# Rotary scores from high and low halves, the mask product first, the value product after the rotary scores

## What is computed

```python
def block(args):
    ql, qr, qp = args
    s = (jnp.einsum('bqhc,bkc->bhqk', ql, c, preferred_element_type=jnp.float32)
         + jnp.einsum('bqhr,bkr->bhqk', qr, kr, preferred_element_type=jnp.float32))
    s = s * ks[:, :, None, :] * scale
    s = jnp.where(k_pos[None, None, None, :] <= qp[None, None, :, None], s, NEG_INF)
    p = jax.nn.softmax(s, axis=-1).astype(c.dtype)
    return jnp.einsum('bhqk,bkc->bqhc', p, c)
...
o = jnp.einsum('bshc,chv->bshv', o, w_uv).reshape(bsz, s_q, N_HEADS * V_DIM)
return o @ w_o
```

## Time and profile before

| | |
|---|---|
| median of 3 runs | 2081.05 us |
| the three runs | 2082.86, 2081.05, 2073.68 us |
| the profiled execution, its own time | 2079.41 us |
| its span in the trace | 2077.7 us |
| busy share of the span: PE, DVE, ACT, POOL | 99%, 77%, 53%, 16% |
| granted TensorE clock, mean | 0.998 |
| sample stage, from the first turned page to the first scores | 1473.6 to 1499.5 us |
| heads, from the first scores to the last rotary scores | 1499.5 to 1674.4 us, with the projection from 1582.6 to 1628.9 us in them |

### The profile page before, as it was taken

The page is one execution under the profiler, slowest core; times in us unless marked ns, Lnnn a source line. Parts: engine busy times, 40 slices in busy tenths (PEclk is TensorE's granted clock), DMA queues, the critical chain, the costliest instruction groups (busy, mean ns, idle before and its releaser), DMA issues.

```text
span 2077.7 us, 44241 instructions
## 1 busy us (share of the span) xinstructions
PE 2058.9 (99%) x16692; PEld 1993.7 (96%) x16692; DVE 1601.1 (77%) x2667; ACT 1103.1 (53%) x1898; POOL 341.7 (16%) x384
## 2 busy tenths in 40 slices
PE   9999999999999999999999999999999999999999
PEld 8999999999999999999999999998768789999998
DVE  6779885437367998988899898678665468989987
ACT  5446554443225655645665665445564346655555
POOL 0011111221011111111211111111122121111111
PEclk9999999999999999999999999999999999999999
DMA  5467783322224777775777777441322127777775
GB/s 162 121 160 179 187 200 105 91 92 80 84 81 114 176 180 179 180 182 151 172 179 181 187 183 172 138 134 29 96 72 82 61 62 158 178 189 171 198 175 129
DMA packets 362555, 293.57 MB, mean 141 GB/s; under 512 B 21591, under 2 KB 329092, under 8 KB 362148
## 3 DMA queue, kind: packets, MB, share of 16 engines
q1 hardware_dynamic: 326266, 226.84, 36.4%
q0 software_dynamic: 35824, 64.37, 19.1%
q10 hardware_dynamic: 314, 0.37, 0.1%
HBM read 224.57 MB, written 2.66 MB: 109 GB/s over the span
## 4 chain that ended last, share of the span: by engine, by line
PE 85%; DMA 8%; DVE 4%; issue 2%; ACT 1%; SPq 1%; ACTq 0%; DVEq 0%
PE side L825 26%; PE main L776 26%; PE main L825 19%; DMA raw<-raw 3%; DMA sums_w<-raw 2%; PE side L1370 2%; DMA raw<-in_ffn_w_gate 2%; PE main L1130 2%; PE main L1300 1%; DVE w_lo L2104 1%; DMA raw<-in_ffn_w_up 1%; PE side L1340 1%; PE side L1220 1%; PE main L1200 1%; PE side L1044 1%
## 5 line engine op out<-in xcount | busy, mean ns | idle before, releaser
L825 PE MATMUL side<-xw_hi,w_hi 128*128 128x260 f32 x1344 | 381.1, 284 | 5.1 <-ACT main L1545 1.5
L825 PE MATMUL side<-xw_hi,w_lo 128*128 128x260 f32 x1344 | 381.0, 283 | 0.0
L825 PE MATMUL side<-xw_lo,w_hi 128*128 128x260 f32 x1344 | 380.1, 283 | 0.0
L2104 DVE TENSOR_TENSOR w_lo<-raw,w_hi 128x512 fp32r<-128x512 f32 (+2 forms) x472 | 323.4, 685 | 35.5 <-ACT w_hi L1490 16.6
L825 PE MATMUL main<-xw_hi,w_hi 128*128 128x260 f32 x1008 | 286.1, 284 | 0.0
L825 PE MATMUL main<-xw_lo,w_hi 128*128 128x260 f32 x1008 | 284.7, 282 | 0.0
L825 PE MATMUL main<-xw_hi,w_lo 128*128 128x260 f32 x1008 | 284.5, 282 | 0.0
L825 PEld LDWEIGHTS side<-xw_hi,w_hi 128*128 128x128 f32 x1344 | 253.2, 188 | 8.5 <-ACT main L1545 3.0
L825 PEld LDWEIGHTS side<-xw_hi,w_lo 128*128 128x128 f32 x1344 | 253.2, 188 | 0.0
L825 PEld LDWEIGHTS side<-xw_lo,w_hi 128*128 128x128 f32 x1344 | 252.8, 188 | 0.0
L2104 DVE TENSOR_TENSOR w_lo<-sums_w,w_hi 128x1024 fp32r<-128x1024 f32 (+1 forms) x232 | 218.6, 942 | 1.0 <-ACT w_hi L1473 1.0
(11 more groups left out here) (460 smaller groups left out, 5340.8 us busy)
## 6 DMA issues: line engine op xcount, KB each, us to landing
sums_w<-raw POOLq DMA_DIRECT2D x112, 256.0 KB, 3.3
raw<-raw POOLq DMA_DIRECT2D x112, 256.0 KB, 5.1
raw<-in_ffn_w_gate SPq DMA_DIRECT2D x86, 256.0 KB, 4.4
raw<-in_ffn_w_gate SPq DMA_DIRECT2D x43, 512.0 KB, 5.9
raw<-in_ffn_w_up SPq DMA_DIRECT2D x84, 256.0 KB, 4.5
raw<-in_ffn_w_up SPq DMA_DIRECT2D x42, 512.0 KB, 6.2
raw<-in_gmlp_w_in SPq DMA_DIRECT2D x16, 1024.0 KB, 5.3
raw<-in_ffn_w_down SPq DMA_DIRECT2D x56, 256.0 KB, 4.1
```

What stands on the lines that cost most here:

```text
L825: mm = nc.tensor.matmul(into[j], w_tiles(w, weights_at(s, j))[:, k, :], moving[:, k, order[j], :], start=(j in (0, 1) and k == 0 and i == ...
L2104: a = nc.vector.tensor_tensor(dst, src, hi.bitcast(F32), ALU.subtract)
```

## The change

The change does the following.

- The rotary scores are made of three fp32r products as the latent ones are. For that there are `kr_hi`, `kr_lo` (the keys, once) and `rope_hi`, `rope_lo` (the queries, once for two heads, all 128 partitions). `rope_lo` takes the place of `qr` in memory, tile by tile.
- `qr_moved` is filled by SP with two DMAs for two heads (partitions 0 to 63 to 64 to 127 and back), where ACT copied 64 partitions in each head. ACT makes `rope_hi` by two copies and POOL `rope_lo` by two subtractions for two heads.
- The first two moves stand on SP ahead of the last 16 page DMAs, the third ahead of the first loads of `w_o`, and the others among the loads of `key_scale`.
- The mask product comes first in each bank.
- The value product comes after all scores of a head, on PE; on DVE the value tile is copied after the maxima.
- A few tiles and semaphores are placed anew (`ks_rows`, `kr_lo`, `c_squared`), which moves no work.

Cut to what matters (the second part of a move, the tiles and the renamed semaphores are left out):

```diff
+            def move_rope(r_):
+
+                if r_ >= 2:
+                    sp.wait_ge(rope_lo_set, 2 * r_ - 2)
+                if r_ >= 1:
+                    sp.wait_ge(qr_moved_set, 32 * r_)
+                for lo in (0, ROPE):
+                    sp.dma_start(qr_moved[lo:lo + ROPE, r_ % 2, :], qr[ROPE - lo:P - lo, r_, P:3 * P]).then_inc(qr_moved_set, 16)
+
             sp.wait_ge(kn_done, 17)
+            sp.wait_ge(qr_set, H // 2)
+            move_rope(0)
+            move_rope(1)
             load_pages(10, 14)
...
             sp.wait_ge(os_done, 2)
+            move_rope(2)
             load_out(0)
             load_out(1)
             for h in range(2, H):
                 spread_scales(h)
+                if h % 2 == 0 and h + 4 < H:
+                    move_rope(h // 2 + 2)
...
+                for blocks in ((2, 3), (0, 1)) if h == 0 else ((0, 1, 2, 3),):
+                    if h == 0 and 0 in blocks:
+                        pe.wait_ge(sd_set, 3)
+                    for q in blocks:
+                        if free is not None and q % 2 == 0:
+                            pe.wait_ge(evac_done, free - 1 + q // 2)
+                        if h >= 1:
+                            pe.wait_ge(score_scaled, QB * (h - 1) + q + 1)
+                        nc.tensor.matmul(main[:, q // 2, q % 2, q * P:(q + 1) * P], mask_ops[:, 0, :], mask_ops[:, 1, :],
+                                         start=True, stop=False, skip_group_check=True)
+                    for q in blocks:
+                        bank = main[:, q // 2, q % 2, :]
+                        nk, cols = (q + 1) * P, slice(q * P, (q + 1) * P)
+                        for a, b in ((q_hi[:, h % 2, cols], c_hi), (q_hi[:, h % 2, cols], c_lo), (q_lo[:, h, cols], c_hi)):
+                            nc.tensor.matmul(bank[:, 0:nk], a, b[:, 0:nk], start=False, stop=False, skip_group_check=True)
+                r_ = h // 2
+                pe.wait_ge(rope_lo_set, 2 * r_ + 2)
+                for pair in ((0, 1), (3, 2)):
+                    for i, (a, b) in enumerate(((rope_hi[:, r_ % 2, :], kr_hi), (rope_hi[:, r_ % 2, :], kr_lo),
+                                                (rope_lo[:, r_, :], kr_hi))):
+                        for q in pair:
...
-                    scores(h, lambda: values(g - 1), free=e if g == KC + 1 else None)
+                    scores(h, free=e if g == KC + 1 else None)
+                if g >= 1:
+                    values(g - 1)
...
+            def round_rope(r_):
+
+                if r_ >= 2:
+                    act.wait_ge(scored, QB * (2 * r_ - 2))
+                act.wait_ge(qr_moved_set, 32 * r_ + 32)
+                nc.scalar.activation(outer_blocks(rope_hi[:, r_ % 2, :]), outer_blocks(qr[:, r_, 0:SEQ]), ACT.Copy)
+                nc.scalar.activation(rope_hi[:, r_ % 2, P:3 * P], qr_moved[:, r_ % 2, :], ACT.Copy).then_inc(rope_hi_set, 1)
...
                 if h + 2 < H:
-                    move_rope(h + 2)
+                    if h % 2 == 0:
+                        round_rope(h // 2 + 1)
                     split_queries(h + 2)
...
-                if g >= 1:
-                    value_tile(g - 1)
                 if h < H:
                     dve.wait_ge(key_scale_in[h % 2], 16 * (h // 2 + 1))
...
+                if g >= 1:
+                    value_tile(g - 1)
                 if g >= 0:
                     dve.wait_ge(prob_turned, 3 * g + 2)
...
+            def rope_rest(r_):
+
+                pool.wait_ge(rope_hi_set, r_ + 1)
+                nc.gpsimd.tensor_tensor(outer_blocks(rope_lo[:, r_, 0:SEQ]), outer_blocks(qr[:, r_, 0:SEQ]),
+                                        outer_blocks(rope_hi[:, r_ % 2, :].bitcast(F32)), ALU.subtract).then_inc(rope_lo_set, 1)
+                nc.gpsimd.tensor_tensor(rope_lo[:, r_, P:3 * P], qr_moved[:, r_ % 2, :],
+                                        rope_hi[:, r_ % 2, P:3 * P].bitcast(F32), ALU.subtract).then_inc(rope_lo_set, 1)
```

More of the change, by code:

```diff
@@ L251, in program @@
         c_lo = sb("c_lo", [P, TOK], F32R, late)
-        qr = sb("qr", [P, H // 2, TOK], F32, late)
+        turned_queries = ExitStack()
+        qr = sb("qr", [P, H // 2, TOK], F32, turned_queries)
+        turned_queries.close()
+        rope_lo = sb("rope_lo", [P, H // 2, TOK], F32R, late)
         wkv = sb("wkv", [P, H, P], F32, late)
@@ L313, in program, with outer_blocks @@
         o_t = sb("o_t", [P, TOK], F32, heads)
+        kr_hi = sb("kr_hi", [P, SEQ], F32R, heads)
+        rope_hi = sb("rope_hi", [P, 2, SEQ], F32R, heads)
         KV_THIRD = -(-H * P // 3)
         qr_moved = rstd_all[:, 0:4 * P].rearrange("p (s c) -> p s c", s=2)
+        def outer_blocks(t):
+            return t.rearrange("p (q c) -> p q c", c=P)[:, 0:QB:QB - 1, :]
         heads.close()
@@ L1269, in _, with scores @@
                     tr.then_inc(ks_turned, 1)
-            def scores(h, between=None, free=None):
+            def scores(h, free=None):
                 if h == 0:
-                    pe.wait_ge(c_lo_set, 1)
+                    pe.wait_ge(c_lo_set, 2)
                     pe.wait_ge(key_parts_set, 2)
                 pe.wait_ge(q_lo_set, h + 1)
-                for q in (2, 3, 0, 1) if h == 0 else range(QB):
-                    if h == 0 and q == 0:
+                for blocks in ((2, 3), (0, 1)) if h == 0 else ((0, 1, 2, 3),):
+                    if h == 0 and 0 in blocks:
@@ L1278, in scores @@
                         pe.wait_ge(sd_set, 3)
-                    if free is not None and q % 2 == 0:
-                        pe.wait_ge(evac_done, free - 1 + q // 2)
-                    if h >= 1:
-                        pe.wait_ge(score_scaled, QB * (h - 1) + q + 1)
-                    bank = main[:, q // 2, q % 2, :]
-                    nk, cols = (q + 1) * P, slice(q * P, (q + 1) * P)
-                    nc.tensor.matmul(bank[:, 0:nk], q_hi[:, h % 2, cols], c_hi[:, 0:nk], start=True, stop=False)
@@ L1286, in scores @@
-                    nc.tensor.matmul(bank[:, 0:nk], q_hi[:, h % 2, cols], c_lo[:, 0:nk], start=False, stop=False)
-                    nc.tensor.matmul(bank[:, 0:nk], q_lo[:, h, cols], c_hi[:, 0:nk], start=False, stop=False)
-                for q in range(QB):
-                    nc.tensor.matmul(main[:, q // 2, q % 2, q * P:(q + 1) * P], mask_ops[:, 0, :], mask_ops[:, 1, :],
-                                     start=False, stop=False, skip_group_check=True)
-                if between is not None:
-                    between()
@@ L1293, in scores @@
-                pe.wait_ge(qr_moved_set, h + 1)
-                for q in (0, 1, 3, 2):
-                    nk = (q + 1) * P
-                    if q in (0, 3):
-                        lo, q_rope = ROPE * (h % 2), qr[:, h // 2, q * P:(q + 1) * P]
-                    else:
-                        lo, q_rope = ROPE - ROPE * (h % 2), qr_moved[:, h % 2, (q - 1) * P:q * P]
-                    nc.tensor.matmul(main[:, q // 2, q % 2, 0:nk], q_rope[lo:lo + ROPE, :],
-                                     kr_t[lo:lo + ROPE, 0:nk], start=False, stop=True).then_inc(scored, 1)
+                    for q in blocks:
[5 more added lines that the diff above has]
+                                         start=True, stop=False, skip_group_check=True)
@@ new lines, in scores @@
+                for pair in ((0, 1), (3, 2)):
+                    for i, (a, b) in enumerate(((rope_hi[:, r_ % 2, :], kr_hi), (rope_hi[:, r_ % 2, :], kr_lo),
+                                                (rope_lo[:, r_, :], kr_hi))):
+                        for q in pair:
+                            lo, nk = ROPE * (h % 2) if q in (0, 3) else ROPE - ROPE * (h % 2), (q + 1) * P
+                            mm = nc.tensor.matmul(main[:, q // 2, q % 2, 0:nk], a[lo:lo + ROPE, q * P:(q + 1) * P],
+                                                  b[lo:lo + ROPE, 0:nk], start=False, stop=(i == 2), skip_group_check=True)
+                            if i == 2:
+                                mm.then_inc(scored, 1)
@@ L1915, in _ @@
             act.wait_ge(evac_done, e + 3)
-            nc.scalar.activation(square[:, 0, :], c_t[:], ACT.Square).then_inc(c_squared, 1)
+            nc.scalar.activation(square[:, 0, :], c_t[:], ACT.Square).then_inc(cq_squared, 1)
             act.wait_ge(rms_mm, at_mla.rms + 3)
@@ L2008, in _ @@
                     nc.scalar.activation(c_hi[:], c_t[:, 0:SEQ], ACT.Copy).then_inc(c_hi_set, 1)
+                if y == 9:
+                    nc.scalar.activation(kr_hi[:], kr_t[:, 0:SEQ], ACT.Copy).then_inc(c_hi_set, 1)
                 if y == 4:
@@ L3165, in _ @@
                     query_rest(h + 2)
+                    if h % 2 == 0:
+                        rope_rest(h // 2 + 1)
             value_rest(H - 1)
```

25 lines of the change are left out of this document (11 added, 14 removed).

## The result

The changed kernel takes 2094.53 us in the median of six runs (2088.77 to 2097.46); the kernel before took 2081.0 us beside it (2073.68 to 2082.86, six runs). The ratio is 1.0076, 95% interval 1.0062 to 1.0089, so the change makes the kernel slower by 0.8%. The forecast was 2085 with a range of 2076 to 2094. The profiled execution took 2095.88 us, its span is 2094.2 us; before it was 2077.7, so 16.5 us are to be found.

What follows compares the result with a forecast made beforehand. PE's own sequence was taken as the bound, other engines counting only where PE waits. Terms of -0.9, +1.2, +1.6, +2.0 and +0.7 gave +4.6 us on 2079.41, 2084.0 (2085.7 by the runs' median); forecast 2085, range 2076 to 2094.

Steps and rivals of the forecast that it cites:

- Rotary scores: PE's rotary stage in each head: three fp32r passes plus 0.1 us for switching, 1.28 becomes 1.06, 0.22 us less.
- The first rival: Array halves don't run side by side for fp32r: rotary stage 2.09 us, +1.0 us in 15 heads, 2100; chance 0.07.
- The rule that the prediction took from the Trainium skill's page: Weight loads overlap running matmuls only from another row group; the rotary stage would take 1.6 us.
- Value tile: PE's last two transposes wait for DVE's copy, weighing starts at T + 2.52; reordering costs 0.15 us per head.
- the maxima end at T + 1.45: On DVE, the third reduction again starts at T + 0.16, so the maxima end at T + 1.45, taken as 1.5.
- T: The moment at which PE leaves a head's rotary scores, 1538.83 in the regular head of the profile before.
- Heads 3 to 6: DVE, with the quarter of `w_lo` in between, is free only at T + 8.0; +1.2 us over four heads.
- the third rival: POOL's new subtractions slow DVE's normalisation; with its room used up, 2.1 us in 6 heads, 2097; chance 0.04.
- SP at the pages: Two moves ahead of the last 16 page DMAs delay them 3.5 us on SP; PE loses 1.6 us.
- SP at head 2: Moves issued first on SP make head 2's key scales late for DVE; heads 1 and 2 together +2.0 us.
- they arrive at 1523.1: Head 2's key scales land at 1523.1 instead of 1522.3, while DVE wants them at 1520.6.
- Head 10: Masks first need all four banks, so PE starts its products only at 1629.96: +0.7 us.

Runs made afterwards that it cites:

- one rotary term less: The changed kernel without the product of the queries' high halves and the keys' low halves in the rotary scores; 2091.28 us, 1.0057.
- the reordering alone: The kernel before with only the value product moved behind the rotary scores on PE and the value tile behind the maxima on DVE; 2084.85 us, 1.0026.

## Why the prediction was wrong

**What bounds the kernel, and the sign.** The forecast of 2085 was slower than before, and the kernel is slower, but "slower" by more than a measurement can tell had a chance of only 0.14, against 0.83 for the same. That PE's own sequence sets the time, and that other engines count only where PE waits, is right for the kernel before. In the new order it failed for the regular heads: each has a wait, and their length is that of a circle over POOL, DVE, PE and ACT that the forecast never summed.

**Rotary scores, "I add 0.1. So 1.28 becomes 1.06".** The halves do run side by side (pairs start as one), and a term costs its columns. The term that was mis-sized is the 0.1 us added to the columns: 0.24 us are fixed. So the stage is 0.06 us shorter and not 0.22. The first rival falls. The rule that the prediction took from the Trainium skill's page "TensorE: Matmul & The Clock Gate", Part 3, "The mechanism", falls too, as it was read there: by it the stage would have taken 1.6 us, and it took 1.22. (The same section also lets a load go ahead into a background weight buffer, which the prediction left out and which the trace doesn't contradict.)

**Value tile, "+0.15", and "the maxima end at T + 1.45".** In head 13, T = 1671.52; the ninth transpose starts at 1673.88 and the weighing at 1674.16, T + 2.64 against my T + 2.52. The size is nearly right; what failed is that I gave the maxima their old 0.17 us. Before, they started after POOL's subtraction had ended (head 6: 1556.36 against 1555.78). With the value tile no longer ahead of them they start inside it. Regular heads became +0.23 instead of -0.07. Along PE's own sequence the difference can be added up, 0.16 in the rotary stage, 0.12 here and the rest at other borders, but that sum is no cause: a stage shorter by another 0.33 us bought nothing (one rotary term less), and the old float32 stage made no head longer (the reordering alone). The step that failed is that PE's terms were added with the maxima ending at T + 1.45; they end when POOL lets them, and the circle through them takes 8.29 us. With POOL's subtraction moved behind them the heads take 8.19.

**Heads 3 to 6.** The step "the quarter of `w_lo` comes in between, and DVE is free at T + 8.0" failed in kind. DVE was free in time: its first reduction starts 0.42 us ahead of T (1556.67 and 1557.09) as in other heads. The quarter delays POOL's `h_lo` by 0.38 us, POOL's next subtraction starts later, and this one holds the maxima. I had the third rival (POOL slows DVE, 0.04) and looked for it at the normalisation, in even heads; it was at the maxima, in twelve of sixteen heads, even and odd, from a subtraction that was there before. (In the old order of the value tile, POOL's new subtractions did hold the maxima, but in odd heads.)

**SP at the pages.** The delay on SP (3.5 forecast; the last page's issue ends at 1487.03 instead of 1483.19, 3.8) and PE's wait (1.6 and 2.01) were nearly right. What was missing is the clock after the wait, 1.7 us.

**SP at head 2.** The step "they arrive at 1523.1" failed, 13.6 us after head 1's start there: the scales left 6.56 us after it (1519.68 and 1513.12) instead of 5.9, flew 9.0 us instead of 7.6, and were there after 15.6. DVE was late by 4.0 us (1528.68 against 0.42 ahead of T, 1524.69) where 2.5 was forecast. And the wait of 4.21 us brought the clock down for the weighing, 2.1 us that no term had.

**Head 10.** Right: 0.7 forecast, 0.8 measured, and its split removed it.

**The range** ended at 2094, half a microsecond below the median. It had no mechanism in which a wait has a price of its own: the two drops of the clock, 3.8 us together, are more than what the median lies outside by. Other sizes were missed too (DVE's lateness in head 2 by 1.5 us, heads 4 to 7 by 1.5), so the clock alone is not the reason.

## What to carry to other kernels

A wait on PE is not priced by its length alone: behind idle times of 1.8 to 4.2 us the next products here ran at half the clock in all cases but one, so a term that makes PE idle needs the lower clock as its upper bound. Where a wait appears, follow it round to the next head: the circle that it closes sets the length, and shortening what is not on it gains nothing. When an operation moves on an engine, lay it against what the neighbour does at its new time, not only against its own queue; the shortest instruction may be the one that is held. And where a small transfer is wanted early, look at what the same queue issues ahead of it: one line moved gave back 6.8 of the 16.5 us in heads 2 and 3.

## What the runs showed of the hardware

- DVE's maxima of two SBUF operands (0.165 us) are held to the end of POOL's subtraction, up to 0.645 us; reductions with one operand in PSUM are not.
- Three fp32r terms on both halves of the array cost 0.33 us each for 768 columns at 2.4 GHz and 0.24 once; four float32 passes of the same columns took 1.28 with nothing on top, so what the 0.24 are for is open.
- The granted clock fell to 0.50 behind idle times of 3.52 to 4.21 us in head 2, of 2.15 there in the old order of the value tile, and in five of six profiles behind 1.80 to 2.67 us at the pages. It stayed at 1.00 behind 1.03, 1.58 and once 1.90 us.
- 256 KB for 128 partitions were there 9.0 us after their issue with two megabytes of loads ahead in the queue, 6.25 us with one, and 3.2 us with none.
